# Trailing sums by doubling on VectorE instead of band matmuls, in a four-layer trunk on eight cores

## What is computed

```python
def pool_mixer(p, buf, start_pos, w_pg, pool_scale):
    pp = jnp.concatenate([buf, p], axis=1)           # 15 earlier rows in front
    for gi, w in enumerate((2, 4, 8, 16)):           # 4 groups of 128 channels
        mean = (sum of the last w rows of pp[..., group gi]) / min(pos + 1, w)
        d = mean - p[..., group gi]
        outs.append(d @ w_pg[gi])
    return concat(outs) * pool_scale, pp[:, -15:]    # also the new state
```

## Time and profile before

| what | us |
|---|---|
| median of three executions | 2159.1 (2158.25 to 2368.44) |
| the profiled execution | 2153.68 |
| its span, first to last instruction of the slowest core (core 6) | 2152.6 |
| spans of the eight cores | 2143.1 to 2152.6 |
| TensorE busy / VectorE / ScalarE / GpSimd | 2075.5 / 995.7 / 725.0 / 595.4 |

### The profile page before, as it was taken

One profiled execution on the slowest core, in us unless ns is written; L12 is line 12 of the kernel. 1 busy time (PEld: TensorE's weight loads), 2 busy tenths in 40 slices (PEclk: granted clock), 3 DMA queues, 4 the chain that ended last, 5 costly groups with the idle time before them and its releaser, 6 DMA issues.

```text
span 2152.6 us, 39389 instructions; the slowest of 8 cores (2143.1 to 2152.6 us)
## 1 busy us (share of the span) xinstructions
PE 2075.5 (96%) x13248; PEld 1231.1 (57%) x13248; DVE 995.7 (46%) x1529; ACT 725.0 (34%) x1681; POOL 595.4 (28%) x1117
## 2 busy tenths in 40 slices
PE   3999999999999999999999999999999999999998
PEld 1565565466556546645655664565575575575674
DVE  2354344435434443643544454354455455355454
ACT  2323423423342242333234233322423423433431
POOL 3322411321242132223214222321421422422420
PEclk9999999999999999999999999999999999999999
DMA  9974588187468758737753881885696695794881
GB/s 211 171 112 79 92 128 132 38 138 108 69 114 124 125 163 128 118 50 131 123 98 60 135 131 37 147 130 128 145 181 114 111 175 95 126 171 83 134 145 52
DMA packets 118812, 255.69 MB, mean 119 GB/s; under 512 B 16516, under 2 KB 18628, under 8 KB 115352
## 3 DMA queue, kind: packets, MB, share of 16 engines
q0 software_dynamic: 103664, 210.02, 62.2%
q1 hardware_dynamic: 14952, 43.14, 6.1%
HBM read 451.02 MB, written 12.99 MB: 216 GB/s over the span
## 4 chain that ended last, share of the span: by engine, by line
PE 85%; DVE 4%; POOL 3%; issue 3%; ACT 2%; DMA 2%; ACTq 0%; SPq 0%; DVEq 0%; POOLq 0%
PE ps L872 33%; PE ps L619 17%; PE ps L805 8%; PE ps L816 8%; PE ps L566 5%; PE ps L774 5%; PE ps L590 3%; POOL sb_stats L420 2%; ACT sb_scr L401 2%; DVE sb_scr L409 2%; DMA sb_xg<-x_p 2%; DVE sb_xg L405 2%; POOL sb_stats L418 1%; PE ps L839 1%; PE ps L834 1%
## 5 line engine op out<-in xcount | busy, mean ns | idle before, releaser
L872 PE MATMUL ps<-sb_hT,sb_ring 128*128 128x384 bf16 (+1 forms) x4608 | 709.8, 317 | 0.0
L401 ACT ACTIVATE sb_scr<-ps 128x384 f32<-128x384 f32 (+4 forms) x760 | 409.4, 549 | 839.3 <-PE ps L805 266.1
L872 PEld LDWEIGHTS ps<-sb_hT,sb_ring 128*128 128x128 bf16 x4608 | 449.5, 98 | 256.2
L366 POOL DMA_DIRECT2D sb_ring<-w_in x504 | 269.5, 547 | 945.9 <-PE ps L872 519.2
L619 PE MATMUL ps<-sb_woutb,sb_mix 128*128 128x512 bf16 x2176 | 475.9, 379 | 0.6 <-ACT sb_cxb L401 0.6
L619 PEld LDWEIGHTS ps<-sb_woutb,sb_mix 128*128 128x128 bf16 x2176 | 211.2, 98 | 250.7 <-issue 1.3
L405 DVE TENSOR_TENSOR sb_scr<-ps,sb_scr 128x384 f32<-128x384 f32 (+1 forms) x288 | 153.1, 532 | 256.3 <-PE ps L816 256.2
L409 DVE SCALAR_TENSOR_TENSOR sb_scr<-sb_cxb,sb_convw,sb_scr 128x384 f32<-128x384 f32 (+1 forms) x336 | 182.1, 542 | 145.3 <-ACT sb_ccarry L401 108.5
L418 POOL TENSOR_SCALAR sb_stats<-sb_stats 128x1 f32<-128x1 f32 x204 | 77.9, 382 | 565.7 <-ACT sb_scr L401 563.1
L566 PE MATMUL ps<-sb_ring,sb_hT 128*128 128x512 bf16 (+1 forms) x1088 | 191.5, 330 | 14.9 <-DVE sb_woutb L409 13.5
L805 PE MATMUL ps<-sb_hT,sb_ring 128*128 128x384 bf16 (+1 forms) x1152 | 200.5, 317 | 0.0
(11 more groups left out here) (64 smaller groups left out, 1473.9 us busy)
## 6 DMA issues: line engine op xcount, KB each, us to landing
sb_ring<-w_in POOLq DMA_DIRECT2D x480, 256.0 KB, 10.0
sb_woutb<-w_out POOLq DMA_DIRECT2D x192, 256.0 KB, 6.9
sb_ring<-w_in POOLq DMA_DIRECT2D x12, 1536.0 KB, 12.4
sb_ring<-w_in POOLq DMA_DIRECT2D x12, 1024.0 KB, 12.7
sb_xg<-x_p SPq DMA_DIRECT2D x16, 512.0 KB, 3.6
y_p<-sb_xg SPq DMA_DIRECT2D x16, 512.0 KB, 2.6
sb_pre_bc<-pre_g SPq DMA_DIRECT2D x12, 512.0 KB, 5.0
sb_post_bc<-post_g SPq DMA_DIRECT2D x12, 512.0 KB, 4.9
```

What stands on the lines that cost most here:

```text
L366: emit(POOL, lambda g: g.dma_start(out=flat, in_=src), writes=a.res, dsem=ds, extra=[prev_tok] if prev_tok else [])
L401: return emit(ACT, lambda a: a.activation(out=out, in_=in_, func=func, scale=scale, **kw), reads=reads, writes=writes)
L872: ins = pe.matmul(bank(b, N), lhsT=wa.ap[:, k, :], rhs=hT[:, k, j0 * 128:j0 * 128 + N], start=(k == 0), stop=(k == 7))
```

## The change

p is projected channel-major (`p_job`), four channel groups with weights of their own in the ring, each followed by its z_b. ScalarE evicts it as float32 into `pbuf` (two buffers, 16 columns of the tiles before in front, which VectorE copies from `pcar`). `pool_vec` then forms the sum over the last w tokens on VectorE by doubling: 1, 2, 3 or 4 additions of the tensor with itself, shifted by 1, 2, 4 and 8 columns, then one operation that scales and subtracts p. In the passes of group 0 the first 16 columns are corrected with 1/min(pos + 1, w). Sample tokens are ordered step by step (all 16 sequences' first token, then the second), so that for them a shift by one token is a shift by 16 columns, with the history in front (`pbs`). The band matrices, `ptm`, `phalo` and `histp` are gone, and only pieces 0 to 4 of w_out wait for the convolution stage. The wpg product of a channel group comes one group later (`wpg_job`), that of the last one inside head 0. The first p and z_b jobs stand behind the third v job. At the start, SyncE loads tile 0, `pre_bc` and tiles 1 and 2, and GpSimd waits for `pre_bc` before it issues v's weights; tiles 3 to 5 wait for v's.

```diff
-    out = [("v", OFF_V, 768), ("p", OFF_P, 512)]
-    out += [(("zb", gi), OFF_ZB + gi * 128, 128) for gi in range(4)]
+    out = [("v0", OFF_V, 512), ("v1", OFF_V + 512, 256)]
+    for gi in range(4):
+        out += [(("p", gi), OFF_P + gi * 128, 128), (("zb", gi), OFF_ZB + gi * 128, 128)]
...
+        def p_job(g, l, gi, si_):
+            sti = GROUPS[g][1][si_]
+            j0, n, is_s = sti
+            pb = gi % 2
+            if si_ == 0:
+                dve_copy(pbuf[:, pb, 0:PH], pcar[:, l * 4 + gi, :], reads=[R["pcar"]], writes=[R_pbuf[pb]])
+            b = alloc_banks()
+            in_job(b, need(wsched[(g, l)][("p", gi)]), sti)
+            Np = np_of(sti)
+            act(pbuf[:, pb, PH + j0 * 128:PH + j0 * 128 + Np], bank(b, Np), AF.Copy,
+                reads=[bank_res[b]], writes=[R_pbuf[pb]])
+            if is_s:
+                act(pbs[:, gi, 15 * SB:23 * SB], ps[:, 512 * b + Np:512 * b + Np + 128], AF.Copy,
+                    reads=[bank_res[b]], writes=[R_pbs[gi]])
...
+        def window_sum(src, n0, n, step, w, R_src, lo):
+            cur, R_cur, off, k = src, R_src, 0, 1
+            buf = 0
+            while k < w:
+                ext = (w - 2 * k) * step
+                a = n0 - ext
+                ln = n + ext
+                dst = pw[:, buf, 0:ln]
+                dve_tt(dst, cur[:, a - off:a - off + ln], cur[:, a - off - k * step:a - off - k * step + ln], ALU.add,
+                       reads=[R_cur], writes=[R_pw[buf]])
+                cur, R_cur, off = pw[:, buf, :], R_pw[buf], a
+                buf ^= 1
+                k *= 2
+            return cur[:, n0 - off:n0 - off + n], R_cur
...
+            sv, R_s = window_sum(src, PH, Np, 1, w, R_pbuf[pb], 0)
+            dve_stt(dv[:, 0:Np], sv, 1.0 / w, src[:, PH:PH + Np], ALU.mult, ALU.subtract,
+                    reads=[R_s, R_pbuf[pb]], writes=[R_scr[d]])
+            if tiles[0] == 0:
+                dve_tt(sv[:, 0:PH], sv[:, 0:PH], icnt[:, gi, :], ALU.mult, reads=[R_s, R["icnt"]], writes=[R_s])
+                dve_tt(dv[:, 0:PH], sv[:, 0:PH], src[:, PH:2 * PH], ALU.subtract,
+                       reads=[R_s, R_pbuf[pb]], writes=[R_scr[d]])
+            dve_copy(pcar[:, l * 4 + gi, :], src[:, Np:Np + PH], reads=[R_pbuf[pb]], writes=[R["pcar"]])
+            if sts[-1][2]:
+                srs = pbs[:, gi, :]
+                sv, R_s = window_sum(srs, 15 * SB, 128, SB, w, R_pbs[gi], 0)
+                dve_stt(dv[:, Np:Np + 128], sv, 1.0 / w, srs[:, 15 * SB:23 * SB], ALU.mult, ALU.subtract,
+                        reads=[R_s, R_pbs[gi]], writes=[R_scr[d]])
...
+                POOL.h.wait_ge(d_par["pre"].sem, 16)
...
-                        ex = [W["p"].res[0].w]
+                        ex = [W["v1"].res[0].w]
...
+            gz_of = {}
+            fill = [lambda: p_job(g, l, 0, 0), lambda: gz_of.__setitem__((0, 0), zb_job(g, l, 0, 0))]
+            if not same_group:
+                while t_pending and t_pending[0] < 2:
                     t_next()
+            while state["v"] < nt:
+                if state["v"] >= 3 and fill:
+                    fill.pop(0)()
+                elif t_pending and (state["v"] not in t_em or len(t_pending) > 1 or not fill):
                     t_next()
+                    v_next() if state["v"] in t_em and state["v"] < 3 else None
                 else:
+                    v_next()
...
+            late = None
             for gi in range(4):
+                for si_ in range(len(sts)):
+                    if (gi, si_) != (0, 0):
+                        p_job(g, l, gi, si_)
+                release(W[("p", gi)])
+                d = pool_vec(g, l, gi)
+                for si_ in range(len(sts)):
+                    if (gi, si_) not in gz_of:
+                        gz_of[(gi, si_)] = zb_job(g, l, gi, si_)
+                release(W[("zb", gi)])
+                if late is not None:
+                    wpg_job(g, l, *late)
+                late = (gi, d, [gz_of[(gi, si_)] for si_ in range(len(sts))])
```

More of the change, by code:

```diff
@@ L37 @@
 CB_ONES = 1
[L38 to L47, removed]
+CB_N = 2
+C32_MASKP = 0
+C32_MASKS = 1
+C32_N = 2
+PH = 16
 def _host_consts():
@@ L585, in vp_job @@
                         reads=[bank_res[b], bank_res[b + 1], R_stat[si], R["vg_bc"]], writes=[R_vn[j]])
-            b = alloc_banks()
-            def pjob(pe):
-                for k in range(8):
-                    ins = pe.matmul(bank(b), lhsT=hT[:, k, j * 128:(j + 1) * 128],
-                                    rhs=W["p"].ap[:, k, :], start=(k == 0), stop=(k == 7))
-                return ins
-            emit(PE, pjob, reads=[R_hT[j]] + W["p"].res, writes=[bank_res[b]])
-            act(ptm[:, j + 1, :], bank(b), AF.Copy, reads=[bank_res[b]], writes=[R_ptm[j + 1]])
@@ new lines, in pool_vec @@
+        def pool_vec(g, l, gi):
+            tiles, sts = GROUPS[g]
+            w = POOL_W[gi]
+            pb = gi % 2
+            Np = sum(np_of(x) for x in sts)
+            d = alloc_scr()
+            dv = scr[:, d, :].bitcast(BF16)
+            src = pbuf[:, pb, :]
+            sv, R_s = window_sum(src, PH, Np, 1, w, R_pbuf[pb], 0)
[11 more added lines that the diff above has]
+                        reads=[R_s, R_pbs[gi]], writes=[R_scr[d]])
+            return d
@@ new lines, in zb_job, with wpg_job @@
+        def zb_job(g, l, gi, si_):
+            sti = GROUPS[g][1][si_]
+            N = sti[1] * 128
+            b = alloc_banks()
+            in_job(b, need(wsched[(g, l)][("zb", gi)]), sti)
+            gz = alloc_scr()
+            act(scr[:, gz, 0:N], bank(b, N), AF.Silu, reads=[bank_res[b]], writes=[R_scr[gz]])
+            return gz
+        def wpg_job(g, l, gi, d, gzs):
+            for si_, sti in enumerate(GROUPS[g][1]):
+                j0, n, _ = sti
+                N = n * 128
+                b = alloc_banks()
+                emit(PE, lambda pe, b=b, N=N, j0=j0: pe.matmul(
+                    bank(b, N), lhsT=wpg[:, l * 4 + gi, :],
+                    rhs=scr[:, d, :].bitcast(BF16)[:, j0 * 128:j0 * 128 + N], start=True, stop=True),
+                    reads=[R_scr[d], R["wpg"]], writes=[bank_res[b]])
+                dve_stt(mix[:, 6 + gi, j0 * 128:j0 * 128 + N], bank(b, N),
+                        pscale[:, l * 4 + gi:l * 4 + gi + 1], scr[:, gzs[si_], 0:N], ALU.mult, ALU.mult,
+                        reads=[bank_res[b], R_scr[gzs[si_]], R["pscale"]], writes=[R_mix[6 + gi][si_]])
@@ L690, in run_pass @@
                         conv_state_out(prev_pass[1])
-                if j < nt and not same_group and not (prev_pass is None and j == 0):
+                if j < nt and not same_group and not (prev_pass is None and j < 3):
                     t = tiles[j]
@@ L922, in run_pass @@
                                 reads=[R_cxb[cb_], R["convw"], R_scr[y]], writes=[R_scr[y]])
-                    for f_ in late:
+                    for f_ in late_c:
                         f_()
```

292 lines of the change are left out of this document (116 added, 176 removed).

## The result

| | kernel before | kernel after |
|---|---|---|
| median of four executions, us | 2158.7 (2155.31 to 2368.44) | 2236.1 (2204.80 to 2401.05) |
| profiled execution, us | 2153.68 | 2206.16 |
| span of its slowest core | 2152.6 | 2205.1 |
| TensorE / VectorE busy | 2075.5 / 995.7 | 2073.1 / 1164.4 |
| TensorE's waits, all kinds | 68.7 | 119.4 |

The ratio is 1.0222 (95%: 1.0192 to 1.0252): slower, by about 2%. For the kernel after these are 2204.8 and 2206.2 us, 7 to 8 above the forecast.

What follows compares the result with a forecast made beforehand. TensorE was taken as the bound, busy 2075.5 of 2152.6 us. Terms -30 - 33 + 63 + 30 + 5 - 3 + 7 = +39 on the median 2159.1 gave 2198; own range 2175 to 2215, full range 2132 to 2228.

Steps and rivals of the forecast that it cites:

- Bands, -30: TensorE's stream: removing 544 band matmuls at 0.055 us each, by their starts in the timeline, saves 30 us.
- The busy row: Band matmuls priced by busy time, 138 ns each, would make 75 us; the forecast rejected this for the starts.
- Old waits, -33: TensorE's existing waits outside the start, together 32.8 us, were to go.
- Pooling stage, +63: New TensorE waits on VectorE's pooling: 4.0, 1.7 and 9.1 us a pass in groups 0, 1, 2, plus 3.8.
- The chain itself: Pooling stage: pooling, scalings, copy, evictions follow without overlap; fourth result at 25.4 us in group 1, 29.7 in group 2.
- the first pass's extra: Very first pass: four setup mask products, 0.96 us each, stand ahead of the pooling on VectorE: 3.8 us.
- The bank waits: Pooling stage: TensorE waits for PSUM banks, 0.6 us a pass in group 1 and 1.1 in group 2.
- Boundary, +30: Pass boundaries: two transposes ahead of the first v wait 2.5 us in 9 passes, 5.7 and 1.5 between groups.
- Start, -3 and +5: Start: first v matmul near 35 against 37.71 wins 2.7 us; late first p job and head 0 cost 5.
- Clock, +7: TensorE's clock: one fall a pass in group 2, after the longer pooling waits, 1.7 us each, 7 us.
- My third rival: The clock falls at every new wait over 2 us: 22 falls, 37 us instead of 7, 2228; chance 0.17.
- a sign against it: Pooling stages: a clock well below 1 there would show the prediction wrong; no size given.

Runs made afterwards that it cites:

- experiment 4: Kernel before with every band matmul issued twice (544 more): 2181.7 us beside 2156.4, ratio 1.0116.
- experiment 2: Kernel after with the 16-column copy that opens pbuf issued one pooling ahead: profiled execution 2158.7 to 2162.7 us, median 2193.3, ratio 1.0172.
- experiment 1: Kernel after with one v job put back between the two transposes at every boundary but the first: 2193.2 us, ratio 1.017.
- experiment 5: Kernel after with eight extra matmuls ahead of the second transpose at each of eleven pass boundaries: 2194.6 to 2196.5 us, ratio 1.0185.
- experiments 3: Kernel after with the start's loads in the old order (v's weights at once, norm vector behind tile 0): 2204.6 and 2204.9 us, ratio 1.0224.
- 6: Kernel after with the transposes of tiles 3 and 4 behind the first v jobs in the very first pass: 2209.0 and 2209.3 us.
- experiment 9: Kernel after, first pass: third transpose, three v jobs, first p and z_b job ahead of tile 3's normalisation, some w_out loads later: 2202.5 to 2203.1 us.
- the eleventh: The tenth with the next pass's first 16-column copy issued ahead and p and z_b jobs between boundary v jobs: 2153.2 to 2156.3 us, ratio 0.9994.
- the tenth: Kernel after with experiment 1, experiment 2 and the early start of experiment 9 together: 2150.6 to 2157.1 us, once 2175.7; ratio 0.9997.

## Why the prediction was right, and where it was off

Direction and places were right. Two terms of the sum were mis-sized, in opposite directions: the waits of the pooling stage (63 for 36.8) and the clock (7 for 27.3).

- **Bands, -30.** Right: -25 to -29 by experiment 4. The busy row (75 us) would have turned the sign of the sum (+39 - 45).
- **Old waits, -33.** Right as a sum of what goes, but one thing was not seen: some 8 us come back in the v stage of group 2 (L554 on hT and woutb, some 2.5 us in three passes).
- **Pooling stage, +63.** The mechanism was right and is shown by experiment 2; the size was 36.8. Group 0 waits 2.4 to 2.6 a pass instead of 4.0, group 1 0.35 to 0.65 instead of 1.7, group 2 some 6.1 (4.4 in its first pass) instead of 9.1, the first pass's extra 2.3 instead of 3.8. The chain itself was nearly right: the fourth result of group 1 came 24.8 us after time 0 for 25.4, that of group 2 after 27.3 for 29.7. A subtraction takes 0.96 and 0.69 us and not 1.02 and 0.75; in group 2, more came from the turns between poolings (scalings, copy, evictions), twice 2.1 us where the forecast has 2.9 and 2.6. Two microseconds of chain are the larger part of a wait of three: a wait is the difference of two long sums, and small errors of both stand in it whole. The bank waits (0.6 and 1.1 a pass) did not come at all.
- **Boundary, +30.** 33.9 measured, 2.32 to 2.44 for 2.5 in nine passes; the second group boundary waits 5.70 where I took 1.5. That the order makes the wait is shown by experiment 1, and its price in clock by experiment 5. In before, v and the token-major p projection (1.73 us a tile) stood between two transposes; channel-major, p can't run before three tiles are transposed. How much of the lost cover was p's is not shown, since no run puts it back. Experiment 1 adds what I had not seen: behind the transposes' wait lies a second one of the same size, for banks that VectorE frees, so that a new order gives back little of it.
- **Start, -3 and +5.** First v at 44.51 and not 35: x3 became ready for its square only at 35.4 us (ScalarE idle for 14.22 us, on the DMA), not some 6.5 after it was issued near 23.3. x3 to x5 took 12.1 to 17.1 us to land. TensorE did not wait for the p weights. In waits it is +3.8 (39.7 for 35.9) for +2. In experiments 3, 6 and 9 neither the loads' order nor the first matmul's time was worth more than 4 us.
- **Clock, +7.** The term most under-sized: "I charge one fall a pass in group 2". There are 17 falls of about 1.65 us; 27.3 us more than before. My third rival had the mechanism (22 falls, 37 us) and I gave it 0.17; its condition was waits over 2 us, and the falls are at them: the six boundaries inside groups 0 and 1 and both between groups, five poolings in group 0, and one a pass in group 2, where in three passes 2.05 us is followed 8 us later by some 3.6 and only the second has one. The three boundaries inside group 2 wait 2.3 us and have none on any core, and in experiment 2 some of the others have none either; what decides stays unexplained. The prediction named a clock well below 1 in pooling stages as a sign against it: nine of the falls lie at the wpg products of that stage, so this sign came in part. Experiment 5 shows cause and price apart from the wait.

The Trainium skill (TensorE: Matmul & The Clock Gate, on oscillation) describes a kernel whose clock drops each time TensorE idles between bursts. The windows around 237 us and experiment 5 agree for waits of 2.3 us and more in groups 0 and 1; the three boundaries inside group 2 (2.3 us), 18 of the 48 in experiment 2 and the boundaries of experiment 1 (two waits of 1.2 to 1.8 us) do not show it.

So +62 of waits for 50.7, +7 of clock for 27.3, and -30 of bands for some -26: +39 for +52.5. After lies at 2205 to 2206, 7 to 8 above the forecast and inside its own range. Part of the closeness is luck: two errors of opposite sign, and a sum put on a median of 2159.1, where the profiled execution of before has 2153.7; put on that, it misses by 13.

## What to carry to other kernels

When a stage hands a buffer from one in-order engine to another and back, look for the cheapest instruction in the ring: here a copy of 0.17 us, issued one pooling later than it could be, cost 42 us of 2205. Price a wait of TensorE with the clock that can follow it, here 1.5 to 1.7 us again behind most waits of 2.4; a few matmuls of no use inside the wait took that part away. And before a projection is moved, ask which waits its matmuls covered where they stood.

## What the runs showed that I had not expected

- Useless work paid: 88 matmuls of 512 columns more, 10 us less (experiment 5).
- Fewer waits can cost as much as more: the eleventh waits 7 us less than the tenth and loses 10.6 us more clock, and is not faster.
- The early v jobs took 18 us off the first v matmul (44.5 to 26.4) and 3 off the end (experiment 9).
- The same wait of 2.3 to 2.4 us is followed by a fall of the clock in one place and not in another, and in one kernel and not in the next (experiment 2). No run here separates what decides.
